# Moving the transposes of x's second quarter behind the first weight unit

## The chip, the cores and the metric

One Trainium2 chip, one of its cores. The metric is device time in microseconds of one launch. TensorE (PE in the profile) multiplies and transposes into the eight PSUM banks; VectorE (DVE) and ScalarE (ACT) work on tiles in SBUF and PSUM; SyncE (SP) issues nearly all loads from HBM; GpSimd (POOL) issues a few small ones. All numbers are f32; matrix products are split in a high and a low part so that three products in fp32r stand for one in f32.

## The reference

A two-layer trunk on x (256 tokens, 2048 channels) with a condition vector c (2048). What matters here is its beginning:

```python
cond = jax.nn.silu(c)
for l in range(DEPTH):                                    # DEPTH = 2
    mod = (cond @ w_ada[l] + b_ada[l])[:, None, :]        # w_ada[l]: 2048 x 12288
    sh1, sc1, g1, sh2, sc2, g2 = jnp.split(mod, 6, axis=-1)
    u = x * (1.0 + sc1) + sh1
    y = even_mixer(u, w_in_ab, ...) if l % 2 == 0 else odd_mixer(u, w_qkv, ...)
    x = layer_norm(ALPHA * x + (1.0 + g1) * y, ...)
    u = x * (1.0 + sc2) + sh2
    y = conv_ffn(u, w_up[l], conv_w[l], conv_b[l], w_down[l])
    x = layer_norm(ALPHA * x + (1.0 + g2) * y, ...)
```

`even_mixer` begins with `z = u @ w_in` (2048 x 5136) and ends with `@ w_out`; between them are a pooling mixer and gated linear attention. So the first weights can be multiplied once the matching channels of u are there, and these need x transposed (channels on partitions) and the sums over all 2048 rows of w_ada for the shift and scale of those channels.

## The kernel before

**Weight units.** All large weights are streamed in units of 4 x 128 rows and 512 columns (1 MB, two loads of 512 KB), through four raw slots. For each unit ScalarE writes a rounded high part (`hi_unit`, L557), VectorE the rest as low part (`lo_unit`, L889), each in two slots, and TensorE does 16 products with the high part (8 with u's high and 8 with u's low part) and 8 with the low part (`unit`, L1353). A unit is a column chunk c and a quarter j of the 2048 rows. The front has 48 units (32 of w_in in `IN_ORDER`, 16 of w_out). Units 0, 1, 2 are quarter 0 of three chunks (banks 0/1, 2/3, 4/5), units 3, 4, 5 are quarter 1 of the same, so unit 3 is the first that needs u's channels 512 to 1023.

**Pieces of u.** x is loaded in four quarters (`load_x`, L484), each 512 KB. A piece v is 256 channels: two pieces to a quarter of x. TensorE transposes a piece (`x_T`, L1601) into bank 7, ScalarE copies it to SBUF (`x_piece`, L614) and later writes u's high part (`u_piece`, L619), VectorE u's low part (`u_first`, L940). Since all pieces share bank 7, a transpose waits for the copy of the piece before.

**Sums over w_ada.** The 24 "pairs" of `ADA_PAIRS` are 1024 columns of w_ada each, 16 rows (r) of 128 x 1024 loaded one by one, 512 KB each, into eight slots. Row r of a pair is multiplied by silu(c) and added up, by VectorE (`ada_row`, L896), or for rows 0 to 11 of pairs 0 and 1 by TensorE (`ada_rows`, L1439): pair 0 in banks 4 and 5, pair 1 in banks 6 and 7, which VectorE reads as it folds in row 12 (L902). `ada_sum` (L1419) then sums over partitions on TensorE into bank 6, and `ada_evac` (L912) adds the bias: pair n gives shift and scale of u's quarter n (n below 4). Pairs 2 and 3 are spread over units 3 to 14, two or three rows a unit (`ada_plan`, L144); pairs 4 and 5 are the first gate's.

**Order around the change.** Each engine's program is in order and written out by hand.

- SyncE: pair 0's rows with x's first quarter after row 3; units 0 and 1; pair 1's rows 0 to 7; unit 2; x's second quarter; pair 1's rows 8 to 15; units 3 to 6 and so on, each followed by the rows that `ada_plan` gives to the unit four before (L499 to L526). A row's load waits until its slot was used by TensorE or VectorE (`load_row`, L405). The load of unit u waits for `lo_unit` of u - 4 (L418), counted from unit 4. Behind unit 9, once the second set of parameter rows is transposed, goes the first gate's bias (`gate_load`, L457): a broadcast of 1 MB into the tile that shares its place with those rows. Behind unit 10 follow the small low-rank gate weights (L516 to L519).
- TensorE: pair 0's rows, pieces 0 and 1, sum of pair 0, then unit 0, pair 1's rows 0 to 7, unit 1, rows 8 to 11, unit 2, pieces 2 and 3, sum of pair 1 (L1700 to L1774), unit 3, unit 4, `rows_T` (L1591) into bank 7, and on. Pieces 4 and 5 follow unit 7, 6 and 7 follow unit 10.
- ScalarE: pieces 0 and 1, high parts 0 and 1, u pieces 0 and 1, high parts 2 and 3, pieces 2 and 3, u pieces 2 and 3, high part 4, and on (L639 to L712).
- VectorE: pair 0, u pieces 0 and 1, low parts 0, 1, 2, pair 1's rows 12 to 15, low part 3, evacuation of pair 1's sum, u's low pieces 2 and 3, low part 4, then low part s + 2 and the rows of unit s for each s (L1215 to L1287).

Elsewhere `layer_norm` and `mlp` follow, and the second layer with attention; none of it is touched.

Of the kernel before, what the change touches and what calls it, by code (L numbers as in the profile page):

```python
# [14 lines left out]
S = 256  # L15
P = 128
F = 5504
KT = D // P
# [171 lines left out]
def build(nc, A, out):  # L190
# [7 lines left out]
    with ctx:  # L198
# [110 lines left out]
        def sem(name):  # L309
            if name not in sems:  # L310
                sems[name] = ctx.enter_context(nc.semaphore(name))
            return sems[name]
# [16 lines left out]
        def ada_slot(m, r):  # L329
# [2 lines left out]
                return r % ADA_FIRST, 2 * m + r // ADA_FIRST + 1  # L332
            return r % ADA_SLOTS, 8 + (m - 4) * (KT // ADA_SLOTS) + r // ADA_SLOTS + 1

        def pe_rows_at(m):
            return pair[2 + m]

# [66 lines left out]
        def _(sp):  # L404
# [94 lines left out]
            for v in range(FRONT_UNITS):  # L499
                c, j = IN_ORDER[v] if v < IN_UNITS else OUT_ORDER[v - IN_UNITS]  # L500
                load_quarter(v, w_in if v < IN_UNITS else w_out, c, j)
                if v == 1:
                    for r in range(ADA_FIRST):
                        load_row(1, r)
                if v == 2:
                    load_x(1)
                    for r in range(ADA_FIRST, KT):
                        load_row(1, r)
                if v in (6, 8):
                    load_x(2 + (v == 8))  # L510
                if v == 9:
                    sp.wait_ge(sem("rows_T"), 2)
                    gate_load(0, 2, 0)
                if v == 10:
                    sp.wait_ge(u_ready, 2 + U_FIRST + 2)
                    sp.dma_start(w_lr[:, :, :], A["w_in_ab"][0][:, OFF_LR:OFF_LR + GRANK].rearrange(  # L516
                        "(k p) n -> p k n", p=P)).then_inc(sem("lr_in"), 16)
                    sp.dma_start(w_g[0:GRANK, :], A["w_gate_lr"][0]).then_inc(sem("gla_in"), 16)
                    sp.dma_start(w_g[GRANK:GRANK + 1, :], A["b_gate"][0:1, :]).then_inc(sem("gla_in"), 16)  # L519
                if v == 20:  # L520
                    sp.wait_ge(a_step, A0 + 4 * KT)
                    sp.dma_start(sums_in[:, :], A["sums"]).then_inc(sem("pool_in"), 16)
                    sp.dma_start(band[:, :, :], A["band"]).then_inc(sem("pool_in"), 16)
                    for g in range(4):
                        sp.dma_start(w_pool[:, g], A["w_pool"][0, g].rearrange("(k p) n -> p k n", p=P)
                                     ).then_inc(sem("pool_in"), 16)  # L526
# [29 lines left out]
        def _(act):  # L556
# [56 lines left out]

            def x_piece(v):  # L614
                act.wait_ge(sem("xT_full"), v + 1)
                nc.scalar.activation(xT[:, 2 * v:2 * v + 2, :], bank[7].rearrange("p (k s) -> p k s", k=2), ACT.Copy
                                     ).then_inc(sem("xT_out"), 1)

            def u_piece(v):  # L619
# [19 lines left out]
            for v in range(2):  # L639
                x_piece(v)  # L640
            hi_unit(0)
            hi_unit(1)
            for v in range(2):
                u_piece(v)
            for s in range(FRONT_UNITS):
                if s == 2:
                    for v in (2, 3):
                        x_piece(v)
                    for v in (2, 3):
                        u_piece(v)  # L650
                hi_unit(s + 2)
# [228 lines left out]
        def _(dve):  # L880
# [332 lines left out]

            out_tail = y_out((0, "out"), True, True, OUT_BANKS, {c: s for s, c in OUT_LAST.items()})
            for s in range(FRONT_UNITS):  # L1215
                if s == 2:
                    ada_evac(1, 0)
                    u_first(1)
                    lo_unit(s + 2)
                    continue  # L1220
                if s in (13, 17):
# [25 lines left out]
                        mix_lo(v)  # L1247
                if s in OUT_LAST:
                    out_tail(OUT_LAST[s])
                if s == 1:  # L1250
                    beside(s)
                if s < FRONT_UNITS - 1:
                    lo_unit(s + 2)
                if s == GATE_SLOT + 1:
# [97 lines left out]
        def _(pe):  # L1352
# [247 lines left out]

            def x_T(v):  # L1601
                pe.wait_ge(sem(f"x_in{v // 2}"), 16)
                if v:
                    pe.wait_ge(sem("xT_out"), v)
                for k in range(2):
                    for t in range(NT):
                        ins = nc.tensor.transpose(bank[7][:, k * S + t * P:k * S + (t + 1) * P],
                                                  x[:, t, (2 * v + k) * P:(2 * v + k + 1) * P], ident)
                ins.then_inc(sem("xT_full"), 1)

# [89 lines left out]
            for u in range(FRONT_UNITS):  # L1700
                if u < IN_UNITS:
                    c, j = IN_ORDER[u]
                    b = PART_BANKS[c] if j < 2 else FULL_BANKS[c]
                    first, last, piece = j % 2 == 0, j % 2 == 1, U_FIRST + 2 * j
                    if j == 0 and PART_CHUNKS.index(c) >= 3:
                        pe.wait_ge(sem("z_part"), PART_CHUNKS.index(c) - 2)
                    if j == 2:
                        n = FULL_CHUNKS.index(c)
                        if n < 2:
                            pe.wait_ge(sem("z_part"), 7 + n)  # L1710
                        else:
                            pe.wait_ge(sem("z_done"), n - 1)
                else:
                    c, j = OUT_ORDER[u - IN_UNITS]
                    b = OUT_BANKS[c]
                    first, last, piece = j == 0, j == 3, U_MIX + 2 * j
                    if j == 0:
                        pe.wait_ge(*((sem("z_done"), 7 + c) if c < 2 else (sem("gla_st"), GH) if c == 2 else
                                     (acc_free, 2 + PH[0, "out"]["chunk"] + 1)))
                unit(u, [(k, 4 * j + k) for k in range(4)], (uhi, ulo), first, last, bank[b:b + 2], piece=piece,  # L1720
                     by_tile=Y_LAST[(0, "out"), 3] if u == FRONT_UNITS - 1 else None)
                if u == 0:
                    pe.wait_ge(sem("xT_out"), 2)
                    pe.wait_ge(a_out, 2)
                    ada_rows(1, 0, ADA_FIRST)
                if u == 1:
                    ada_rows(1, ADA_FIRST, PE_ROWS)
                if u in (2, 7, 10):
                    if u == 2:
                        pe.wait_ge(a_step, A0 + KT + PE_ROWS + 1)  # L1730
                    if u == 7:
                        pe.wait_ge(sem("cols_in"), 2)
                    for v in {2: (2, 3), 7: (4, 5), 10: (6, 7)}[u]:
                        x_T(v)
                if u == 4:
                    pe.wait_ge(sem("rows_in"), 16 * 14)
                    pe.wait_ge(sem("xT_out"), 4)
                    rows_T(2, 14, bank[7])
                if u == LR_SLOT:
                    pe.wait_ge(sem("lr_lo"), 1)  # L1740
                    pe.wait_ge(sem("xT_out"), 8)
                    low_rank(0, 12)
                if u == LR_SLOT + 1:
                    low_rank(12, KT).then_inc(sem("lr"), 1)
                if u == GATE_SLOT:
                    pe.wait_ge(sem("lr_out"), 1)
                    pe.wait_ge(sem("gla_in"), 32)
                    pe.wait_ge(sem("z_part"), 6)
                    for t in range(NT):
                        ins = nc.tensor.matmul(T[t][:, :], lrT[0:GRANK + 1, t * P:(t + 1) * P], w_g[:, :],  # L1750
                                               start=True, stop=True)
                    ins.then_inc(sem("gate_pre"), 1)
                if u in HEAD_S1:
                    if u == 21:
                        pe.wait_ge(sem("log_a"), 1)
                        pe.wait_ge(sem("pool_in"), 16 * 6)
                        pe.wait_ge(sem("z_done"), 2)
                    gla_T(HEAD_S1[u])
                if u in HEAD_S2:
                    gla_scores(HEAD_S2[u])  # L1760
                if u in HEAD_S3:
                    gla_values(HEAD_S3[u])
                for g in POOL_MEAN.get(u, ()):
                    pool_mean(g)
                for g in POOL_MAP.get(u, ()):
                    pool_map(g)
                for v in Y_B_T.get(u, ()):
                    pe.wait_ge(sem("y_b"), v - 3)
                    if v == 5:
                        pe.wait_ge(a_out, 1 + SUM_NO[5, 1] + 1)  # L1770
                    channels_T(lambda t, k: z[:, t, OFF_Q + (k - 8) * P:OFF_Q + (k - 7) * P], bank[7 - v % 2], T_MIX, v)
                if u == 39:
                    pe.wait_ge(t_free, 2 + T_MIX + 8)
                beside(u)  # L1774
# [118 lines left out]
```

## Time and profile before

| | us |
|---|---|
| median of 3 runs | 2323.1 (2319.01 to 2328.11) |
| profiled execution, its own time | 2321.39 |
| its span | 2319.6 |
| PE busy | 2244.5 (97%) |
| DVE busy | 1698.1 (73%) |
| ACT busy | 1006.6 (43%) |
| DMA, mean | 264 GB/s |

In the timeline a line has the start, the duration, the engine, the line of the kernel, the operation with the tiles written and read, their shapes, how many instructions were merged (x), and in brackets how long the engine was idle before and what released it. Times are from the span's start. SPq is SyncE's queue: the duration of a DMA there is the time of its issue alone; the time to its landing is in the view of the DMAs, counted from the issue. In the view of stretches a row has start:end, length, the busy time and instructions of PE, PEld, DVE, ACT and POOL, then TensorE's granted clock as a share of 2.4 GHz, the DMA's busy share and GB/s.

### The profile page before, as it was taken

To read this page: it belongs to the slowest core of one execution; us is meant where nothing else is said; L and a number is where in the kernel's file an instruction comes from. 1 tells how busy PE (TensorE), PEld (TensorE's weight loads), DVE (VectorE), ACT (ScalarE), POOL (GpSimd) and SP (SyncE) were. 2 spreads that over 40 slices of the span, in tenths; PEclk is the share of its full clock that TensorE was granted. 3 is DMA by queue.
4 is the path that set the end of the run, shared out by engine and by line. 5 is a ranking of instruction groups with operands and counts; after the bars stand their busy time and mean duration, and the time that the engine had idled before them with its cause. 6 is when DMAs were issued, how large, how long until landed. Compare 5 with 4: busy or idle time off the path is not lost. (4 is left out here: it accounts for less than half of the span.)

```text
span 2319.6 us, 28131 instructions
## 1 busy us (share of the span) xinstructions
PE 2244.5 (97%) x11321; PEld 1880.4 (81%) x11321; DVE 1698.1 (73%) x1672; ACT 1006.6 (43%) x1001; POOL 8.3 (0%) x19
## 2 busy tenths in 40 slices
PE   7899999999999999999999999999999999999996
PEld 3777777788888888888878888887888888888885
DVE  3799889959977778788887667775599645656555
ACT  1445343354443344453355444434544434444432
POOL 1000000000000000000000000000000000000000
PEclk9999999999999999999999999999999999999998
DMA  9999688958778988879967777774688556565553
GB/s 374 362 405 344 242 295 316 346 178 309 276 259 308 306 284 274 283 265 322 341 232 288 272 253 277 276 246 147 219 289 298 205 195 204 185 196 185 192 192 125
DMA packets 392227, 612.66 MB, mean 264 GB/s; under 512 B 21113, under 2 KB 205073, under 8 KB 390562
## 3 DMA queue, kind: packets, MB, share of 16 engines
q1 hardware_dynamic: 389378, 608.42, 74.9%
q10 hardware_dynamic: 2272, 2.20, 0.3%
q8 instruction: 89, 1.46, 0.2%
q0 software_dynamic: 448, 0.25, 0.0%
q14 instruction: 40, 0.33, 0.0%
HBM read 608.70 MB, written 2.10 MB: 263 GB/s over the span
## 5 line engine op out<-in xcount | busy, mean ns | idle before, releaser
L893 DVE TENSOR_TENSOR w_lo<-w_raw,w_hi 128x2048 fp32r<-128x2048 f32 x380 | 847.7, 2232 | 415.8 <-ACT w_hi L562 349.3
L562 ACT ACTIVATE w_hi<-w_raw 128x2048 fp32r<-128x2048 f32 x380 | 710.3, 1870 | 859.2 <-PE banks L1370 520.6
L1486 PE MATMUL banks<-u_hl,w_hi 128*128 128x512 f32 x2368 | 576.6, 392 | 8.7 <-DVE g_sum L1102 6.9
L1486 PEld LDWEIGHTS banks<-u_hl,w_hi 128*128 128x128 f32 x2368 | 432.6, 188 | 96.1 <-DVE g_sum L1102 9.4
L1370 PE MATMUL banks<-w_hi,u_hl 128*128 128x512 f32 x1920 | 481.5, 404 | 11.7 <-ACT u_hl L624 5.9
L1370 PEld LDWEIGHTS banks<-w_hi,u_hl 128*128 128x128 f32 x1920 | 365.1, 193 | 96.4 <-issue 17.3
L1494 PEld LDWEIGHTS banks<-u_hl,w_lo 128*128 128x128 f32 x2368 | 308.6, 191 | 14.5
L1494 PE MATMUL banks<-u_hl,w_lo 128*128 128x256 f32 x2368 | 313.0, 283 | 0.0
L1370 PE MATMUL banks<-w_hi,hid_hi 128*128 128x512 f32 x688 | 269.7, 392 | 0.0
L1370 PE MATMUL banks<-w_hi,hid_lo 128*128 128x512 f32 x688 | 267.8, 389 | 0.0
L909 DVE SCALAR_TENSOR_TENSOR ada_acc<-ada_w,silu_c,ada_acc 128x1024 f32<-128x1024 f32 x187 | 239.2, 1279 | 18.8 <-DMA ada_w<-in_w_ada 12.2
L1370 PE MATMUL banks<-w_lo,u_hl 128*128 128x512 f32 x960 | 238.6, 391 | 3.1 <-DVE w_lo L893 3.1
L1370 PEld LDWEIGHTS banks<-w_lo,u_hl 128*128 128x128 f32 x960 | 180.5, 188 | 41.5 <-DVE w_lo L893 3.9
L1370 PE MATMUL banks<-w_lo,hid_hi 128*128 128x512 f32 x688 | 171.9, 389 | 0.0
L1370 PEld LDWEIGHTS banks<-w_hi,hid_hi 128*128 128x128 f32 x688 | 129.2, 188 | 27.6 <-issue 1.0
L1370 PEld LDWEIGHTS banks<-w_hi,hid_lo 128*128 128x128 f32 x688 | 129.2, 188 | 27.6 <-issue 1.0
L1370 PEld LDWEIGHTS banks<-w_lo,hid_hi 128*128 128x128 f32 x688 | 129.1, 188 | 26.8
L909 DVE SCALAR_TENSOR_TENSOR ada_acc_aux<-ada_w,silu_c,ada_acc_aux 128x1024 f32<-128x1024 f32 x75 | 95.9, 1279 | 2.1 <-DMA ada_w<-in_w_ada 1.1
L792 ACT ACTIVATE conv<-conv 128x512 f32<-128x512 f32 (+1 forms) x44 | 27.4, 623 | 135.8 <-DVE conv L1121 135.8
L909 DVE SCALAR_TENSOR_TENSOR ada_acc_alt<-ada_w,silu_c,ada_acc_alt 128x1024 f32<-128x1024 f32 x52 | 66.7, 1282 | 7.0 <-DMA ada_w<-in_w_ada 3.7
L1121 DVE SCALAR_TENSOR_TENSOR conv<-g_sum,cols,conv 128x255 f32<-128x255 f32 (+1 forms) x148 | 64.9, 479 | 1.3
L586 ACT ACTIVATE g_sum<-banks 128x512 f32<-128x512 f32 (+1 forms) x38 | 22.3, 586 | 97.4 <-PE banks L1494 97.4
(211 smaller groups left out, 1271.8 us busy)
## 6 DMA issues: line engine op xcount, KB each, us to landing
ada_w<-in_w_ada SPq DMA_DIRECT2D x352, 512.0 KB, 6.8
w_raw<-in_w_up SPq DMA_DIRECT2D x344, 512.0 KB, 4.6
w_raw<-in_w_down SPq DMA_DIRECT2D x152, 512.0 KB, 4.7
w_raw<-in_w_qkv SPq DMA_DIRECT2D x96, 512.0 KB, 4.7
w_raw<-in_w_in_ab SPq DMA_DIRECT2D x64, 512.0 KB, 8.8
ada_w_more<-in_w_ada SPq DMA_DIRECT2D x32, 512.0 KB, 10.3
w_raw<-in_w_out_ab SPq DMA_DIRECT2D x32, 512.0 KB, 5.3
w_raw<-in_w_o SPq DMA_DIRECT2D x32, 512.0 KB, 5.1
```

What stands on the lines that cost most here:

```text
L562: nc.scalar.activation(whi[:, u % HL_SLOTS, 0:width], raw[:, u % RAW_SLOTS, 0:width], ACT.Copy).then_inc(w_hi, 1)
L586: nc.scalar.activation(g_sum[:, 0:nf, :], pair[b // 2][:, 0:nf, S:2 * S], ACT.Copy).then_inc(g_low, 1)
L792: nc.scalar.activation(gc[:, 0:nf, :], gc[:, 0:nf, :], ACT.Gelu_apprx_tanh).then_inc(h_gelu, 1)
L893: nc.vector.tensor_tensor(wlo[:, u % HL_SLOTS, 0:width], raw[:, u % RAW_SLOTS, 0:width], whi[:, u % HL_SLOTS, 0:width].bitcast(f32), ALU.s ...
L909: nc.vector.scalar_tensor_tensor(acc[:, :], w, silu_c[:, r:r + 1], acc[:, :], ALU.mult, ALU.add).then_inc(a_step, 1)
L1121: ins = nc.vector.scalar_tensor_tensor(gc[:, k, lag:S], src, cols[:, at:at + 1], gc[:, k, lag:S], ALU.mult, ALU.add)
L1370: return nc.tensor.matmul(banks[t][:, 0:width], u_at(kt, t), w[:, slot, k * width:(k + 1) * width], start=start, stop=stop)
L1486: ins = nc.tensor.matmul(bank[banks[s] + i][:, :], tile(whi, k, s, i), uhl[:, kt].rearrange("p a s -> p (a s)"), start=first and k == 0, s ...
L1494: ins = nc.tensor.matmul(bank[banks[s] + i][:, S:2 * S], tile(wlo, k, s, i), uhi[:, kt, :], start=False, stop=last and k == len(kts) - 1)
```

## The change

Pieces 2 and 3 of x are transposed right behind unit 0, ahead of pair 1's rows, into banks 4 and 5 (`x_bank`), without a wait for the copies of the pieces before; TensorE waits for their copies before unit 2, which accumulates in those banks. ScalarE copies them ahead of high part 2, and writes u pieces 0 and 1 ahead of high part 1. On VectorE the evacuation of pair 1's sum and u's low pieces 2 and 3 go ahead of low part 3. The wait for bank 7's release by VectorE goes from unit 2 to the parameter rows behind unit 4. The gate's bias is loaded behind unit 18 (and the rows of unit 14, the last of pair 3) and not behind unit 9.

```diff
--- before.py
+++ after.py
@@ -332,6 +332,9 @@
                 return r % ADA_FIRST, 2 * m + r // ADA_FIRST + 1
             return r % ADA_SLOTS, 8 + (m - 4) * (KT // ADA_SLOTS) + r // ADA_SLOTS + 1
 
+        def x_bank(v):
+            return T[v - 2] if v in (2, 3) else bank[7]
+
         def pe_rows_at(m):
             return pair[2 + m]
 
@@ -508,7 +511,7 @@
                         load_row(1, r)
                 if v in (6, 8):
                     load_x(2 + (v == 8))
-                if v == 9:
+                if v == 18:
                     sp.wait_ge(sem("rows_T"), 2)
                     gate_load(0, 2, 0)
                 if v == 10:
@@ -613,7 +616,7 @@
 
             def x_piece(v):
                 act.wait_ge(sem("xT_full"), v + 1)
-                nc.scalar.activation(xT[:, 2 * v:2 * v + 2, :], bank[7].rearrange("p (k s) -> p k s", k=2), ACT.Copy
+                nc.scalar.activation(xT[:, 2 * v:2 * v + 2, :], x_bank(v).rearrange("p (k s) -> p k s", k=2), ACT.Copy
                                      ).then_inc(sem("xT_out"), 1)
 
             def u_piece(v):
@@ -639,13 +642,14 @@
             for v in range(2):
                 x_piece(v)
             hi_unit(0)
-            hi_unit(1)
             for v in range(2):
                 u_piece(v)
+            hi_unit(1)
             for s in range(FRONT_UNITS):
-                if s == 2:
+                if s == 0:
                     for v in (2, 3):
                         x_piece(v)
+                if s == 2:
                     for v in (2, 3):
                         u_piece(v)
                 hi_unit(s + 2)
@@ -1213,9 +1217,11 @@
 
             out_tail = y_out((0, "out"), True, True, OUT_BANKS, {c: s for s, c in OUT_LAST.items()})
             for s in range(FRONT_UNITS):
-                if s == 2:
+                if s == 1:
+                    beside(s)
                     ada_evac(1, 0)
                     u_first(1)
+                if s in (1, 2):
                     lo_unit(s + 2)
                     continue
                 if s in (13, 17):
@@ -1247,8 +1253,6 @@
                         mix_lo(v)
                 if s in OUT_LAST:
                     out_tail(OUT_LAST[s])
-                if s == 1:
-                    beside(s)
                 if s < FRONT_UNITS - 1:
                     lo_unit(s + 2)
                 if s == GATE_SLOT + 1:
@@ -1600,11 +1604,11 @@
 
             def x_T(v):
                 pe.wait_ge(sem(f"x_in{v // 2}"), 16)
-                if v:
+                if v and v not in (2, 3):
                     pe.wait_ge(sem("xT_out"), v)
                 for k in range(2):
                     for t in range(NT):
-                        ins = nc.tensor.transpose(bank[7][:, k * S + t * P:k * S + (t + 1) * P],
+                        ins = nc.tensor.transpose(x_bank(v)[:, k * S + t * P:k * S + (t + 1) * P],
                                                   x[:, t, (2 * v + k) * P:(2 * v + k + 1) * P], ident)
                 ins.then_inc(sem("xT_full"), 1)
 
@@ -1722,19 +1726,20 @@
                 if u == 0:
                     pe.wait_ge(sem("xT_out"), 2)
                     pe.wait_ge(a_out, 2)
+                    x_T(2)
+                    x_T(3)
                     ada_rows(1, 0, ADA_FIRST)
                 if u == 1:
                     ada_rows(1, ADA_FIRST, PE_ROWS)
-                if u in (2, 7, 10):
-                    if u == 2:
-                        pe.wait_ge(a_step, A0 + KT + PE_ROWS + 1)
+                    pe.wait_ge(sem("xT_out"), 4)
+                if u in (7, 10):
                     if u == 7:
                         pe.wait_ge(sem("cols_in"), 2)
-                    for v in {2: (2, 3), 7: (4, 5), 10: (6, 7)}[u]:
+                    for v in {7: (4, 5), 10: (6, 7)}[u]:
                         x_T(v)
                 if u == 4:
                     pe.wait_ge(sem("rows_in"), 16 * 14)
-                    pe.wait_ge(sem("xT_out"), 4)
+                    pe.wait_ge(a_step, A0 + KT + PE_ROWS + 1)
                     rows_T(2, 14, bank[7])
                 if u == LR_SLOT:
                     pe.wait_ge(sem("lr_lo"), 1)
```

## Rows read from the trace of the kernel before

**Rows 1.** The page: span, and the DMA's busy share in 40 slices.

```profile
span 2319.6 us, 28131 instructions
...
DMA  9999688958778988879967777774688556565553
```

**Rows 2.** Stretches of 10 us; columns as in the heading line, granted clock third from last.

```profile
60.00:70.00 10.00, 5.73 (x29) 5.22 (x27) 4.47 (x7) 3.93 (x5) 0.00 (x0) 0.68 1.05 406
110.00:120.00 10.00, 9.96 (x47) 8.04 (x45) 8.40 (x6) 4.80 (x4) 0.00 (x0) 1.00 1.04 396
140.00:150.00 10.00, 9.05 (x40) 6.86 (x39) 9.76 (x14) 6.71 (x9) 0.00 (x0) 1.00 1.05 408
270.00:280.00 10.00, 10.00 (x46) 6.70 (x45) 8.52 (x17) 1.92 (x1) 0.00 (x0) 1.00 0.54 191
```

**Rows 3.** The timeline, 60 to 78 us: start, duration, engine, line, tiles, idle before.

```profile
61.92 1.91 ACT L562 ACTIVATE w_hi<-w_raw 128x2048 fp32r<-128x2048 f32 x1 [12.20 <-DMA w_raw<-in_w_in_ab]
...
64.46 1.09 PE L1607 MATMUL banks<-consts,x_tok 128*128 128x128 f32 x4 [3.03 <-ACT x_T L616]
...
65.34 3.41 PE L1435 MATMUL banks<-consts,ada_acc_alt 128*128 128x1 f32 x16
...
68.87 0.15 DVE L925 SCALAR_TENSOR_TENSOR mod<-banks,cols 128x4 f32<-128x4 f32 x1
69.06 2.08 ACT L624 ACTIVATE u_hl<-x_T,mod 128x256 fp32r<-128x256 f32 x4 [2.88 <-DVE mod L925]
...
70.29 5.52 PE L1370 MATMUL banks<-w_hi,u_hl 128*128 128x512 f32 x16 [1.54 <-ACT u_hl L624]
...
77.46 3.79 PE L1370 MATMUL banks<-w_hi,u_hl 128*128 128x512 f32 x16
```

**Rows 4.** The timeline of SyncE's DMA issues, 20 to 110 us.

```profile
37.21 1.68 SPq L485 DMA_DIRECT2D x_tok<-in_x  x1
44.79 1.90 SPq L415 DMA_DIRECT2D ada_w<-in_w_ada  x4
...
66.18 0.88 SPq L420 DMA_DIRECT2D w_raw<-in_w_in_ab  x2
...
84.20 0.34 SPq L460 DMA_DIRECT2D gate<-in_b_ada  x1
...
94.25 8.18 SPq L518 DMA_DIRECT2D w_gate<-in_w_gate_lr  x1
...
102.84 1.21 SPq L420 DMA_DIRECT2D w_raw<-in_w_in_ab  x2
```

**Rows 5.** Issue to landing: x's second load alone, then all weight loads to 100 us.

```profile
x_tok<-in_x SPq DMA_DIRECT2D x1, 512.0 KB, 11.9
...
DMA to landing us min/median/max: 3.9/10.5/13.0
```

**Rows 6.** The timeline, 30 to 61 us.

```profile
30.32 1.95 PE L1435 MATMUL banks<-consts,ada_acc 128*128 128x1 f32 x16 [1.01 <-DVE ada_acc L909]
...
43.69 1.92 PE L1446 MATMUL banks<-ada_w,silu_wide 128*32 128x512 f32 x16
...
47.27 3.92 PE L1370 MATMUL banks<-w_hi,u_hl 128*128 128x512 f32 x16
...
59.70 1.30 PE L1370 MATMUL banks<-w_lo,u_hl 128*128 128x512 f32 x5
59.72 1.28 DVE L909 SCALAR_TENSOR_TENSOR ada_acc_alt<-ada_w_more,silu_c,ada_acc_alt 128x1024 f32<-128x1024 f32 x1
```

**Rows 7.** The timeline, 110 to 150 us.

```profile
110.93 2.67 DVE L909 SCALAR_TENSOR_TENSOR ada_acc<-ada_w_more,silu_c,ada_acc 128x1024 f32<-128x1024 f32 x2 [4.67 <-DMA ada_w_more<-in_w_ada]
...
113.52 2.28 DVE L893 TENSOR_TENSOR w_lo<-w_raw,w_hi 128x2048 fp32r<-128x2048 f32 x1
...
117.55 1.98 PE L1370 MATMUL banks<-w_lo,u_hl 128*128 128x512 f32 x8
...
149.88 2.11 PE L1370 MATMUL banks<-w_lo,u_hl 128*128 128x512 f32 x8 [0.95 <-DVE w_lo L893]
```

## The prediction

> **What bounds the kernel now.** The page first: its span, 2319.6 us, and the DMA's row of tenths [rows 1]. Almost everywhere the DMA engines have room, but in the first slices (58 us each) they have none. The stretches show the same more closely [rows 2]: at 60 to 70 us TensorE is busy 5.7 of 10 us at a granted clock of 0.68 while the DMA moves 406 GB/s; at 140 to 150 us DMA and VectorE (9.8 of 10) are both full; by 270 us TensorE is full and the DMA half empty. So from some 250 us on, the end moves with TensorE's start, and whatever is won or lost ahead of that goes through to the end unless a wait behind it takes it up. At 406 GB/s one 512 KB load takes 0.524/0.406 = 1.29 us; this is the unit of the sums below.
>
> The stall that the change aims at stands in the timeline [rows 3]. Unit 2's last low product ends at 61.0 us, and so does VectorE's last row of pair 1 [rows 6]. The transposes of x pieces 2 and 3 share bank 7, and the copy of piece 2 queues on ScalarE behind the high part of weight unit 3, whose load has only just landed (61.92). So the second transposes start at 64.46, the sum of pair 1 behind them takes 3.41 us at the half clock, the scale is there at 69.02, and unit 3 starts at 70.29: 9.3 us after unit 2's end. Its 16 high products then take 5.52 us, since they too start at the half clock (3.92 for unit 1's [rows 6]).
>
> **What each part costs.** *The transposes move ahead of pair 1's rows.* This decides. x's second load is issued at 37.21 and lands 11.9 us later, at 49.1 [rows 4, 5]. It lies behind a full queue, and the change moves nothing ahead of it. TensorE ends unit 0 at 43.7 and takes pair 1's rows at once [rows 6]. With the change it stands before x_T(2), which waits for that load, and everything behind it on TensorE waits too: 49.1 - 43.7 = 5.4 us, more by 1.9 since unit 0 itself starts earlier (below). After such an idle time the clock will be at the lower level, as at 64.46, where four transposes took 1.09 us [rows 3]: two pieces are 2.2 us, until 51.3.
>
> Then follow TensorE's own steps. Eight rows of pair 1: before from 43.69 to 47.27, 3.6 us, plus 0.9 if the first two run at half clock: 55.8. Unit 1: high part 3.9, low part 1.98 with 0.2 of overlap [rows 6, 7], 5.7: 61.5. Four rows, half of the 3.6: 63.3. Unit 2, 5.7: 69.0. VectorE takes rows 12 to 15 from 63.6 at 1.28 to 1.33 us each [rows 6] and is done at 69.0 as well. The sum takes 1.95 us at the full clock [rows 6]: 71.0. Evacuation 0.25, then 1.2 from the scale to unit 3's first product (69.02 to 70.29): 72.5. Unit 3 at the full clock is 5.7 again, so unit 4 starts near 78.3, where it started at 77.46 [rows 3]. TensorE's whole gain from the shorter sum, the full clock and the missing wait for ScalarE is thus used up by the wait for x: net +0.8 us. With transposes at the full clock and no slow rows it would be -1.2.
>
> *The queue behind those rows.* SyncE issues in order, and its next loads (rows 8 to 15 of pair 1) wait until TensorE has used rows 0 to 7. The first is now issued at 44.79, 1.1 us after TensorE's start [rows 4, 6], while the queue still has work to 49.1. With the change it is issued at 51.3 + 1.1 + 0.5 (one row more slowly) = 52.9, into an empty queue. An almost empty queue took at least 3.9 us to land a load [rows 5], so it lands at 56.8, where by the pace it landed at 49.1 + 1.29 = 50.4. Every load behind it is 6.4 us later; with no slow clock 4.8.
>
> The Trainium skill, DMA: Bandwidth & Descriptors, "Anatomy of one DMA", gives for another queue kind 2.0 us plus bytes over 436 GB/s, an estimate of 3.2 us for this load. By it the delay would be 0.7 us less; the row's 3.9 is what I use.
>
> *The sum ahead of unit 3's low part.* lo_unit(3) now stands on VectorE behind the sum's evacuation and four u parts. These end 2.8 us after the scale, so the low part ends at 71.2 + 2.8 + 2.3 = 76.3, just before unit 3's high products end. TensorE does not wait. But SyncE's load of unit 7 waits for it: 66.18 before [rows 4], 76.3 now. The delayed queue runs to 50.4 + 16 x 1.29 + 6.4 = 77.4 (16 loads lie between), so the new load lands at 76.3 + 3.9 = 80.2 and its second half at 81.5, against 50.4 + 18 x 1.29 = 73.6: the delay grows to about 8.
>
> *The gate rows.* Their load is 1 MB, two loads' time, 2.6 us, taken out of the queue at 84.2 [rows 4]. Delay 5.4. The old queue had holes in this stretch too: from 73.6 to the small gate weights lie 21 loads and one of a quarter of the size, by the pace 27.4 us, so 101.0, but SyncE, held by the 8.18 us issue ahead of unit 11's load, was free only at 102.4 [rows 4]. Of these 1.4 us, or with the last landing twice as much, some may be caught up: 2.6 to 5.4 of delay are left at unit 11's load. I take the middle, 4.0. At the new place, behind unit 18's load, the 2.6 us fall on rows of pair 4, two to a unit and needed beside the low-rank products, which cover them; without that cover they cost up to 2.6. I take 0.
>
> *ScalarE's order.* u pieces 0 and 1 go ahead of unit 1's high part: unit 0 starts 1.9 us sooner, and the time ends in the wait for x. Copies of pieces 2 and 3 now hold unit 2's high part until about 52; unit 2 starts at 63.3. Banks 4 and 5 are free by then, so the new wait before unit 2 costs nothing. All zero.
>
> *Where the delay surfaces.* VectorE at 110.93 has waited 4.67 us for a row of pair 2, and the low part of unit 10 behind it ends at 115.80; TensorE wants it at 117.55 [rows 7]. That is 1.75 of slack, plus the 0.8 above: a delay of 4.0 costs TensorE another 1.4 there. At 149.88 there is none: TensorE waits 0.95 for VectorE already [rows 7], and between the two the DMA is full [rows 2]. So the whole delay is through by unit 15. **Sum:** +4 us on the profiled execution's 2321.4. The median of the runs is 1.7 above that; on it, 2327. What a measurement of this kernel can tell from no change is about 0.5%, 11.6 us.
>
> **Rivals.** *The stall simply goes* (0.22). If the wait for x is shorter than its row says or the hole in the queue is caught up by 110 us, only the quicker sum and the clock are left: unit 3 would start at 61.0 + 1.95 + 0.25 + 1.2, but not before high part 3 (63.83) and its u piece (1.1), so near 65 to 66, 4 to 5 us early: 2318.5. For it speaks that the 9.3 us gap is real. Against it speaks the landing at 49.1, which nothing in the change moves. The skill's DMA page ("Queues, rings and completion order") says that completion isn't in order of issue; the trace shows 11.9 us all the same.
>
> *A wash* (0.24). TensorE loses 0 to 1 at unit 3 and the queue's delay is caught up in its holes and by the gate rows: 2323 to 2324. Holes of that size are there from 75 to 90 us; but slack at unit 10 is 1.75 only.
>
> *Slower beyond noise* (0.06). VectorE's chain of rows carries the delay undiminished: 8 at unit 7, nothing caught up, and the gate's 2.6 us land between pair 4's rows while VectorE is full; a stall there long enough to drop the clock adds 1 to 2. 8 + 2.6 + 1.5 = 12 us: 2335. The point is unit 15's low part: it would have to come 8 us late, not 4. Against it: the gate's 1 MB does leave the queue before unit 10.
>
> *The gate move does nothing* (0.03). Were its load served beside the others at no cost, the delay stays at 8: 2331.
>
> My case holds 0.45. **How the numbers follow.** Cases of -5 to 0 us (0.46) and 3 to 8 (0.48) both lie within 0.5%. The range goes from the stall gone, 2318, to a delay of 8 with some scatter of the runs (they spread by 9 us), 2333; my own case's is 2324 to 2331. Faster by over 0.5% needs more than the stall holds: 0.03. Slower: 0.06.
>
> **What would show it.** Right: the first x_T(2) transpose at 49.1 or a little after, with TensorE idle from 42 at the half clock behind it; rows 8 to 15 issued near 53; GB/s falling for 2 to 5 us around 50 to 55; the sum at 2 us instead of 3.4; unit 3 starting at 71 to 73; low part 10 later than 118 and a wait for VectorE at units 10 to 15. Wrong: transposes at 44, no hole in the DMA's row, unit 3 at 66. If the hole is there but unit 15 is on time, the wash is right.

## The result and the profile after

| | kernel before | changed kernel |
|---|---|---|
| median of 20 runs each, us | 2321.93 | 2328.16 |
| ratio of the two | | 1.0028 (95%: 1.0019 to 1.0037) |
| profiled execution: own time, span, us | 2321.39, 2319.6 | 2328.41, 2326.6 |

The change costs 6.5 us, between 4.4 and 8.6 by the interval. That is slower beyond the runs' scatter, and inside half a per cent.

The page of the changed kernel, span and DMA's busy tenths, to set against [rows 1]:

```profile
span 2326.6 us, 28129 instructions
...
DMA  8999688958878988888967777774688556566553
```

The first slice has 8 where it had 9; of the others a few differ by one, either way. Stretches of the changed kernel (columns as in [rows 2]):

```profile
40.00:50.00 10.00, 2.37 (x12) 1.90 (x11) 0.00 (x0) 0.34 (x1) 0.00 (x0) 0.68 0.68 263
50.00:60.00 10.00, 10.00 (x54) 4.81 (x53) 2.29 (x1) 2.65 (x3) 0.00 (x0) 0.81 0.63 198
100.00:110.00 10.00, 8.66 (x43) 7.04 (x42) 9.61 (x7) 5.70 (x6) 0.00 (x0) 1.00 0.88 279
110.00:120.00 10.00, 8.50 (x38) 6.72 (x36) 5.73 (x4) 2.89 (x3) 0.00 (x0) 1.00 1.02 362
140.00:150.00 10.00, 8.07 (x36) 6.12 (x34) 9.58 (x11) 3.96 (x6) 0.00 (x0) 1.00 1.05 407
270.00:280.00 10.00, 10.00 (x48) 7.20 (x47) 8.43 (x12) 1.95 (x2) 0.00 (x0) 1.00 0.49 171
```

From 40 to 60 us the DMA moved 263 and 198 GB/s, where it has work for 406. At 110 to 120 TensorE is busy 8.5 us instead of 9.96. By 270 us all is as it was. Single microseconds show the hole itself:

```profile
46.00:47.00 1.00, 0.00 (x0) 0.00 (x0) 0.00 (x0) 0.00 (x0) 0.00 (x0) 0.50 0.38 145
48.00:49.00 1.00, 0.46 (x3) 0.49 (x4) 0.00 (x0) 0.00 (x0) 0.00 (x0) 0.50 0.01 2
52.00:53.00 1.00, 1.00 (x12) 0.22 (x8) 0.06 (x1) 0.91 (x1) 0.00 (x0) 0.50 0.00 0
53.00:54.00 1.00, 1.00 (x12) 0.29 (x8) 1.00 (x1) 0.00 (x0) 0.00 (x0) 0.59 0.50 74
```

From 46.4 us on only a trickle moves, the last 0.08 MB before 48.4, and then nothing until 53.2: some 7 us in which the DMA engines have next to no work. TensorE's granted clock is 0.50 there, its lower level. The timeline of the changed kernel, to set against [rows 3, 4, 6]:

```profile
48.54 1.94 PE L1611 MATMUL banks<-consts,x_tok 128*128 128x128 f32 x8 [7.63 <-DMA x_tok<-in_x]
...
50.41 3.59 PE L1450 MATMUL banks<-ada_w,silu_wide 128*32 128x512 f32 x16
...
52.37 2.55 SPq L418 DMA_DIRECT2D ada_w<-in_w_ada  x4
...
63.48 1.28 DVE L906 SCALAR_TENSOR_TENSOR ada_acc_alt<-ada_w_more,silu_c,banks 128x1024 f32<-128x1024 f32 x1 [8.25 <-PE banks L1450]
...
68.99 1.95 PE L1439 MATMUL banks<-consts,ada_acc_alt 128*128 128x1 f32 x16
69.21 1.91 ACT L565 ACTIVATE w_hi<-w_raw 128x2048 fp32r<-128x2048 f32 x1 [16.30 <-DMA w_raw<-in_w_in_ab]
...
71.05 0.15 DVE L929 SCALAR_TENSOR_TENSOR mod<-banks,cols 128x4 f32<-128x4 f32 x1
...
72.47 3.92 PE L1374 MATMUL banks<-w_hi,u_hl 128*128 128x512 f32 x16 [1.54 <-ACT u_hl L627]
...
76.27 0.88 SPq L423 DMA_DIRECT2D w_raw<-in_w_in_ab  x2
...
78.27 3.80 PE L1374 MATMUL banks<-w_hi,u_hl 128*128 128x512 f32 x16
```

TensorE stands 7.63 us until x lands (48.54), transposes at the lower clock, and only behind its rows can SyncE issue pair 1's rows 8 to 15: at 52.37, where it was 44.79. The sum takes 1.95 us and not 3.41, unit 3's high products 3.92 and not 5.52; and still unit 4 starts at 78.27 instead of 77.46. The load of unit 7 leaves at 76.27, 10 us later than before. It waits for unit 3's low part, and unit 3's weights themselves land only at 69.21 (61.92 before): 7.3 of the 10 us are the late queue, and VectorE's new order can account for 2.8 at most. Further on, against [rows 4, 7]:

```profile
99.40 7.89 SPq L521 DMA_DIRECT2D w_gate<-in_w_gate_lr  x1
...
107.70 0.91 SPq L423 DMA_DIRECT2D w_raw<-in_w_in_ab  x2
...
115.03 1.28 DVE L913 SCALAR_TENSOR_TENSOR ada_acc<-ada_w_more,silu_c,ada_acc 128x1024 f32<-128x1024 f32 x1 [3.90 <-DMA ada_w_more<-in_w_ada]
...
117.89 2.28 DVE L897 TENSOR_TENSOR w_lo<-w_raw,w_hi 128x2048 fp32r<-128x2048 f32 x1
...
120.23 2.13 PE L1374 MATMUL banks<-w_lo,u_hl 128*128 128x512 f32 x8 [1.73 <-DVE w_lo L897]
...
148.82 0.54 SPq L463 DMA_DIRECT2D gate<-in_b_ada  x1
...
149.97 3.93 PE L1374 MATMUL banks<-w_hi,u_hl 128*128 128x512 f32 x16 [1.93 <-ACT w_hi L565]
...
154.85 2.14 PE L1374 MATMUL banks<-w_lo,u_hl 128*128 128x512 f32 x8 [0.95 <-DVE w_lo L897]
```

VectorE waits 3.90 us for a row and ends low part 10 at 120.2; TensorE waits 1.73 us for it. The next wait that the kernel before did not have is at unit 15, 1.93 us for its high part (149.97); the 0.95 us ahead of its low products stood there before too. These start at 154.85, where they started at 149.88. The lag of 5.0 us then stands unchanged to 330 us.

### The profile page after: what moved, and what is told of

The parts are those of the page before. It is cut to its first block and busy times, and to the rows that moved or that the text cites. A ratio compares the mean times of both kernels' runs of the same rounds, so it can differ in the third digit from the quotient of the medians.

```text
span 2326.6 us, 28129 instructions
## 1 busy us (share of the span) xinstructions
PE 2244.9 (96%) x11321; PEld 1878.9 (81%) x11321; DVE 1698.4 (73%) x1672; ACT 1006.5 (43%) x1001; POOL 8.4 (0%) x19
```

## The experiments

All comparisons with the kernel before are from runs on the same chip. In the table, "unit 7" is the issue of its load, "GB/s" the DMA's mean from 40 to 80 us, "lag" the start of unit 15's low products less 149.88 (below zero: earlier than before), all three from one profiled execution; the ratio is that of all runs.

| kernel | unit 7 | GB/s | lag | ratio (95%) |
|---|---|---|---|---|
| before | 66.18 | 386 | 0 | 1 |
| changed | 76.27 | 309 | 5.0 | 1.0028 (1.0019 to 1.0037) |
| e1_x_early | 68.52 | 388 | -3.3 | 0.9991 (0.9982 to 0.9999) |
| e2_x_behind_rows | 69.69 | 371 | -1.3 | 0.9994 (0.9986 to 1.0003) |
| e3_unit3_fills | 76.37 | 311 | 5.3 | 1.0015 (1.0006 to 1.0025) |
| e4_gate_back | 76.70 | 308 | 7.6 | 1.0035 (1.0023 to 1.0047) |
| e5_gate_alone | 65.31 | 391 | -2.0 | 0.9995 (0.9984 to 1.0006) |
| e6_lo3_behind_sum | 71.69 | 356 | 3.1 | 1.0024 (1.0013 to 1.0036) |
| e7_x_early_lo3_ahead | 69.78 | 377 | 0.1 | 0.9989 (0.9978 to 1.0000) |
| e8_fill_and_lo3_first | 68.41 | 342 | 3.9 | 1.0006 (0.9996 to 1.0017) |
| e9_x_early_small_on_act | 73.25 | 364 | -2.2 | 0.9970 (0.9959 to 0.9980) |
| e10_small_on_act_alone | 65.83 | 394 | -2.9 | 0.9993 (0.9982 to 1.0003) |
| e11_changed_again | 78.81 | 310 | 7.2 | (one run) |
| e12_e9_lo3_ahead | 65.64 | 406 | -4.7 | 0.9982 (0.9971 to 0.9992) |

One caution on the single profiles. From 5 to 40 us the DMA moved 393 to 397 GB/s in most of them, but 372 in e7's and e11's, 379 in e8's and 366 in e9's. By that alone I estimate all that follows to be late: (394 - 372) x 35 / 406 = 1.9 us in e7 and e11, 1.3 in e8, 2.4 in e9. Their lags are to be read less by about so much; the profiles of e7, e8 and e9 are also each of the slowest run of their kernel.

**x earlier.** In SyncE's program, at unit 1 (and the load at unit 2 taken out):

```diff
                 if v == 1:
+                    load_x(1)
                     for r in range(ADA_FIRST):
                         load_row(1, r)
```

> The changed kernel, but x's second quarter is loaded ahead of pair 1's rows (right behind unit 1's weights) and not behind unit 2's. Theory (the wait for this load stalls TensorE and, through pair 1's rows, dries the load queue): x lands near 36 us, ahead of unit 0's end at 41; no idle wait ahead of the transposes, no hole in the DMA's row near 47 to 53, unit 3 starts at 65 instead of 72.5, the whole is 4 to 5 us faster than the kernel before (ratio 0.998) and 10 to 12 faster than the changed one. Rival (the new order on VectorE or the gate load's new place is what costs): the whole stays 5 to 7 us slower than before. Second rival (the early transposes cost only what TensorE idles, 7.6 us, of which most is covered): within 2 us of before.

The timeline of e1_x_early, TensorE's rows and SyncE's among them:

```profile
60.84 1.95 PE L1439 MATMUL banks<-consts,ada_acc_alt 128*128 128x1 f32 x16
...
64.72 5.49 PE L1374 MATMUL banks<-w_hi,u_hl 128*128 128x512 f32 x16 [1.94 <-ACT u_hl L627]
...
68.52 0.88 SPq L423 DMA_DIRECT2D w_raw<-in_w_in_ab  x2
...
71.86 3.79 PE L1374 MATMUL banks<-w_hi,u_hl 128*128 128x512 f32 x16
...
146.55 2.11 PE L1374 MATMUL banks<-w_lo,u_hl 128*128 128x512 f32 x8 [0.95 <-DVE w_lo L897]
```

The idle wait for x and the hole from 46 us on are gone; a short one stays at 68 to 70 us, where unit 7's load waits for the low part of unit 3. Unit 3 starts at 64.72, unit 4 at 71.86: 5.6 us ahead of the kernel before, a little more than expected. At unit 15's low products its lead is 3.3 us, and the whole gains 2.1 (0.2 to 4.2). So the late x is what makes the change slow; of the expected gain half is missing at the end. TensorE still leads by 5.4 us at unit 14's low products (137.67, before 143.04). It loses 2 us at unit 15, where it waits 1.95 us for the high part: VectorE, ahead of it in that chain, was only 3.3 us early, and had waited 4.8 us for rows of w_ada from 103 to 115 us, behind the hole that the small loads make (below).

**The transposes behind rows 0 to 7.** The calls of `x_T(2)` and `x_T(3)` change places with `ada_rows(1, 0, ADA_FIRST)`.

> The changed kernel, but TensorE does pair 1's rows 0 to 7 ahead of the two transposed pieces, so SyncE's next loads do not hang on x. Theory: TensorE still idles for x, from 44.5 to 48.5, but rows 8 to 15 are issued from 42 on and the queue never runs dry; unit 3 starts near 67.3, 3 us ahead of the kernel before; unit 7's load, held by the low part of unit 3, lands some 3 us later than before and the gate's move gives 2.6 back. Whole: 2 us faster than before (between 0 and 3.5). Rival (it is TensorE's idle time that costs, not the queue): 3 to 4 us slower than before, half of the changed kernel's loss.

The timeline of e2_x_behind_rows, TensorE's rows and SyncE's among them:

```profile
48.28 1.09 PE L1611 MATMUL banks<-consts,x_tok 128*128 128x128 f32 x8 [1.67 <-DMA x_tok<-in_x]
...
65.89 3.96 PE L1374 MATMUL banks<-w_hi,u_hl 128*128 128x512 f32 x16 [1.53 <-ACT u_hl L627]
...
69.69 0.88 SPq L423 DMA_DIRECT2D w_raw<-in_w_in_ab  x2
...
148.54 2.11 PE L1374 MATMUL banks<-w_lo,u_hl 128*128 128x512 f32 x8 [0.41 <-DVE w_lo L897]
```

TensorE waits 1.67 us for x, SyncE's rows go out in time, unit 3 starts 4.4 us early and the loss is gone: 0.9994. A hole remains, since unit 7's load waits for low part 3; the whole comes out near no change, 1.4 us faster (between 3.3 faster and 0.7 slower). TensorE's idle time shrank as well, so e2 alone doesn't separate it from the queue; e6 below does.

**Unit 3's weights fill the hole.** They are loaded behind `load_x(1)`, ahead of rows 8 to 15.

> The changed kernel, but unit 3's weights (1 MB, no wait in their way) are loaded ahead of pair 1's rows 8 to 15, so that they fill 2.6 us of the hole in the queue. TensorE's chain (wait for x, rows, units 1 and 2, sum) stays: unit 3 starts at 72.5 as in the changed kernel. Theory (the delay of the queue, surfacing at units 10 to 15, sets the loss): 2 to 2.6 us faster than the changed kernel, so 4 slower than before. Rival (TensorE's own chain up to unit 3 sets the loss): the same time as the changed kernel, 6 to 7 slower than before.

The timeline of e3_unit3_fills, TensorE's rows and SyncE's among them:

```profile
72.58 3.96 PE L1376 MATMUL banks<-w_hi,u_hl 128*128 128x512 f32 x16 [1.54 <-ACT u_hl L629]
...
76.37 0.88 SPq L423 DMA_DIRECT2D w_raw<-in_w_in_ab  x2
...
155.17 2.12 PE L1376 MATMUL banks<-w_lo,u_hl 128*128 128x512 f32 x8 [0.96 <-DVE w_lo L899]
```

By the profile the rival holds: unit 15 lags 5.3 us, as in the changed kernel. But it is not TensorE's chain either. The 2.6 us of filled hole came back as a second one: unit 7's load could not go before 76.37, and the mean from 40 to 80 us is 311 GB/s as it was 309. The median is 3.5 us above that of before (1.4 to 5.8), near the 4 of the theory and lower than the profile's lag, with an interval that overlaps that of the changed kernel: the median and the profile speak for different sides here.

**Both holes.** e3 with VectorE's low part of unit 3 ahead of pair 1's rows:

```diff
                 if s == 1:
+                    lo_unit(s + 2)
                     beside(s)
                     ada_evac(1, 0)
                     u_first(1)
+                    continue
```

> e3_unit3_fills with one thing more: VectorE does the low part of unit 3 ahead of pair 1's rows 12 to 15 (its high part is ready at 61.5 there), so that SyncE's load of unit 7 no longer waits for the sum to be read. In e3 the filled 2.6 us came back as a second hole, since unit 7's load went out at 76.4 as in the changed kernel. Theory (what is lost is the time that the load queue stands empty up to some 80 us, in however many holes, less the gate's 2.6): unit 7's load goes out near 66 to 68, the first hole keeps 4.3 us, and unit 15 is 1.7 us later than in the kernel before, against 5.3 in e3; the whole 1.5 to 3 us slower than before. Rival (TensorE's late start at unit 3 is enough): unit 15 stays 5 us late.

The timeline of e8_fill_and_lo3_first, TensorE's rows and SyncE's among them:

```profile
68.41 2.87 SPq L423 DMA_DIRECT2D w_raw<-in_w_in_ab  x2
...
81.54 3.79 PE L1378 MATMUL banks<-w_hi,u_hl 128*128 128x512 f32 x16
```

Unit 7's load went at 68.41, in an execution in which x landed 1.7 us later than in the changed kernel's. The lag of 3.9 less 1.3 for the slow head is 2.6, where theory said 1.7 and the rival 5; the whole is 1.4 us slower than before (-0.9 to 3.9). The median speaks for the theory. The profile can't decide: TensorE itself was 4.1 us late at unit 4 in that execution, and a lag of 3.9 at unit 15 is that lateness carried on.

**VectorE's order alone**, on the kernel before: evacuation and u pieces ahead of low part 3, as in the change.

> The kernel before with VectorE's order alone changed: pair 1's sum read and u's low pieces 2 and 3 ahead of the low part of unit 3. TensorE's unit 3 starts at 70.3 as before and does not wait for the low part (ready at 74, wanted at 75.6). But SyncE's load of unit 7 goes out at 74.1 and not 66.2, while the queue is empty at 69 to 71: everything behind is some 5 us late. Theory: 3 to 5 us slower than before, with a wait of TensorE for VectorE at unit 10. Rival (the queue catches up in its holes from 75 to 90 us): within 1 us of before.

The timeline of e6_lo3_behind_sum, TensorE's rows and SyncE's among them:

```profile
67.90 6.17 PE L1370 MATMUL banks<-w_hi,u_hl 128*128 128x512 f32 x16 [1.54 <-ACT u_hl L624]
...
71.69 0.88 SPq L420 DMA_DIRECT2D w_raw<-in_w_in_ab  x2
...
75.74 3.79 PE L1370 MATMUL banks<-w_hi,u_hl 128*128 128x512 f32 x16
...
152.95 2.11 PE L1370 MATMUL banks<-w_lo,u_hl 128*128 128x512 f32 x8 [0.96 <-DVE w_lo L893]
```

Unit 7's load 5.5 us late, 356 GB/s, unit 15 3.1 us late, the whole 5.6 us slower (3.0 to 8.4). This part, which I had given no cost of its own on TensorE and only the last 2 us of the queue's delay, costs by itself nearly as much as the whole change. This run separates the two engines most cleanly: unit 3 starts 2.4 us and unit 4 1.7 us earlier than in the kernel before (70.3 was expected for unit 3), so TensorE had a lead, and unit 15 is late all the same. The load queue set it. In e6 the queue is dry from 70 to 72 us. In the changed kernel it runs so late that this second hole is only a dip, to 209 GB/s at 76 to 77 us; e3, which shortens the first, opens it again. So the two costs don't add.

**The gate's load.** e4 puts it back behind unit 9 in the changed kernel (`if v == 9`), e5 moves it alone in the kernel before (`if v == 18`).

> The changed kernel, but the gate's bias is loaded behind unit 9 as before. Theory: its 2.6 us come back into the delayed queue ahead of unit 10: low part 10 and unit 15 are 2.6 us later than in the changed kernel, the whole is 8 to 9 us slower than the kernel before. Rival (the gate's place does not matter, holes of the queue take it up): as the changed kernel, 6 to 7 us slower. Second rival (its new place collides with pair 4's rows): 4 us slower than before, less than the changed kernel.

> The kernel before with the gate's load alone moved behind unit 18. Theory: the queue is 2.6 us ahead at unit 11, VectorE waits less for pair 2's last rows, but TensorE's start at unit 3 is unchanged, so only its waits at units 14 and 15 (0.4 and 0.95 us) can go: 0 to 1.5 us faster than before. Rival (the rows' queue sets TensorE's time there): 2.6 us faster. Rival (collision with pair 4's rows): 1 to 2 us slower.

Back at unit 9 it costs 2.6 us at unit 15 (7.6 against 5.0), as its bytes say. TensorE was 2.8 us later at unit 4 there than in the changed kernel, but it waits 1.32 us at unit 10 and 1.88 at unit 15, so that is not what sets unit 15. The whole is 8.1 us slower than before. Alone, it makes unit 15 2.0 us early, more than TensorE's two waits there (1.4), with 0.5 from an earlier unit 4 in that execution; on the whole 1.2 us, not told from nothing. So where the queue sets nothing, TensorE's place at unit 4 less these 1.4 us gives its place at unit 15.

**The sum's place with an early x.** e7 is e1 with the old order of `lo_unit(3)` on VectorE.

> As e1_x_early (x's second quarter loaded ahead of pair 1's rows), but with the low part of unit 3 ahead of the sum's evacuation on VectorE, as in the kernel before. With it unit 7's load goes out near 65.5 and not 69 to 70, but u's scale is read up to 2 us later. Theory (the load of unit 7 matters where the queue would run dry, and at 70 us it just does): 0 to 1 us faster than e1_x_early, 4 to 6 faster than before. Rival (the sum's reading decides, as the change says): 1 to 2 us slower than e1_x_early.

The timeline of e7_x_early_lo3_ahead, 63 to 76 us:

```profile
63.62 1.95 PE L1439 MATMUL banks<-consts,ada_acc_alt 128*128 128x1 f32 x16 [0.22 <-DVE ada_acc_alt L913]
65.52 1.91 ACT L565 ACTIVATE w_hi<-w_raw 128x2048 fp32r<-128x2048 f32 x1 [12.54 <-DMA w_raw<-in_w_in_ab]
67.46 2.29 DVE L897 TENSOR_TENSOR w_lo<-w_raw,w_hi 128x2048 fp32r<-128x2048 f32 x1 [3.90 <-ACT w_hi L565]
...
69.75 0.15 DVE L929 SCALAR_TENSOR_TENSOR mod<-banks,cols 128x4 f32<-128x4 f32 x1
...
71.17 5.01 PE L1374 MATMUL banks<-w_hi,u_hl 128*128 128x512 f32 x12 [5.61 <-ACT u_hl L627]
```

VectorE waits for unit 3's high part, so the scale is ready at 69.90, though the sum had ended near 65.6. TensorE waits 5.61 us. The whole takes the time of e1 all the same (2.6 us faster than before, 0.0 to 5.1, where 4 to 6 were expected). The queue would hide what TensorE loses, which e12 below tests.

**The small loads.** SyncE's three gate-weight loads go to ScalarE, behind pieces 4 and 5, `w_lr` last: in e9 on top of e1, in e10 alone.

```diff
+                if s == 7:
+                    act.wait_ge(u_ready, 2 + U_FIRST + 2)
+                    act.dma_start(w_g[0:GRANK, :], ...).then_inc(sem("gla_in"), 16)
+                    act.dma_start(w_g[GRANK:GRANK + 1, :], ...).then_inc(sem("gla_in"), 16)
+                    act.dma_start(w_lr[:, :, :], ...).then_inc(sem("lr_in"), 16)
```

> e1_x_early with the three small gate-weight loads issued by ScalarE behind unit 7's pieces and not by SyncE behind unit 10, where they held SyncE 8 us and emptied the queue. e1 was 5.6 us early at unit 4 and kept 3.1 at unit 15. Theory (the load queue bounds the stretch up to unit 15): with the hole near 100 to 105 gone unit 15 keeps 5 to 5.5 us, the whole is 4 to 5.5 us faster than before. Rival (VectorE's own work, 2 to 3 rows and a low part a unit, takes the lead away): 3 us at unit 15, the whole as e1, 2 faster than before.

> The kernel before with the three small gate-weight loads alone on ScalarE's queue. The hole near 102 to 105 us goes, which is 3 to 4 us of the queue, but TensorE has only its waits at units 14 and 15 (1.4 us) to gain: 1 to 2 us early at unit 15 as in e5_gate_alone, the whole 1 to 2 faster. Rival (nothing to gain): the same. If ScalarE's queue is served slowly and w_lr comes late, TensorE waits at unit 17: slower.

The stretch from 100 to 110 us, of the kernel before:

```profile
100.00:110.00 10.00, 8.65 (x43) 7.08 (x42) 6.04 (x4) 4.92 (x6) 0.00 (x0) 1.00 0.84 245
```

Of e9:

```profile
100.00:110.00 10.00, 8.64 (x42) 7.09 (x41) 9.09 (x7) 3.91 (x5) 0.00 (x0) 1.00 1.07 399
```

The hole that the 8.18 us issue made is gone. e9 is the best kernel of the study: 0.9970, 7.0 us faster than before (4.6 to 9.5), more than expected. Its profile is of its slowest run, with a slow head; less 2.4 its lead at unit 15 is 4.6 us by estimate. Alone the same edit gives 1.6 us, not told from nothing. In its profile unit 15 is 2.9 us early, more than the 1 to 2 expected, but unit 4 was 1.5 us early in that execution already: without an earlier TensorE there is little for the queue to feed.

**e9 with the old order**, to see whether the queue hid TensorE's loss in e7:

> e9_x_early_small_on_act with the low part of unit 3 ahead of the sum's evacuation on VectorE, as in the kernel before (e7 is the same edit on e1). There unit 3 started 3.8 us after the scale could have been read, because the low part waited for its weights, and yet e7's time was that of e1. Theory (in e1 and e7 the load queue bounds the stretch to unit 15 and hides TensorE's start; with the hole at 100 us gone TensorE's own lead counts): 2 to 4 us slower than e9, so 3 to 5 faster than before. Rival (the queue or VectorE still bounds it): the same as e9, 6 to 7 faster than before.

The timeline of e12, and its stretch from 100 to 110 us:

```profile
63.32 2.29 DVE L897 TENSOR_TENSOR w_lo<-w_raw,w_hi 128x2048 fp32r<-128x2048 f32 x1 [2.85 <-ACT w_hi L559]
...
67.02 5.54 PE L1374 MATMUL banks<-w_hi,u_hl 128*128 128x512 f32 x16 [4.55 <-ACT u_hl L621]
...
74.22 3.79 PE L1374 MATMUL banks<-w_hi,u_hl 128*128 128x512 f32 x16
...
100.00:110.00 10.00, 10.00 (x46) 8.27 (x45) 8.42 (x6) 3.37 (x3) 0.00 (x0) 1.00 1.07 393
```

Unit 3 starts at 67.02, 2.3 us behind e1's. The whole is 4.2 us faster than before (1.9 to 6.7), 2.8 less than e9, as theory said. Unit 4 at 74.22 is 3.2 us early; with the 1.4 us of waits gone that gives the 4.7 at unit 15, and VectorE waits for no load from 108 to 141 us. The same sum on e1's 5.6 us would give 7.0, e9's median. But e9's own profile doesn't show it (unit 4 only 1.0 us early, unit 15 2.2), and the intervals of e9 and e12 overlap, so this speaks for the theory more than it proves it.

**The changed kernel once more.**

> The changed kernel once more, for a second profile. In the first the lag behind the kernel before was 5.0 us from unit 15 to 330 us and 7.0 at the end; the 2 us more came with longer half-clock stretches at the layer norms (402 and 436 us). Theory: the lag at unit 15 is again 5 (within 0.5), the further 2 us are scatter of where half-clock stretches fall and come out otherwise, between -2 and +3. Rival: they are part of the change and come again as 2.

Lag at unit 15 7.2, less 1.9 for the slow head 5.3: as in the first. Behind it came another 2.7 us by the end, so this run does not rule the rival out. But between unit 15 and the end the other kernels moved against the same profile of before by anything from -3.7 (e3) to +4.7 us (e7), four of the eleven by +1 to +3. Whether that one profile was a lucky one behind unit 15 or kernels differ there isn't settled.

## Why the prediction was right

Forecast: 2327, no change beyond half a per cent, +4 us. Measured: 2328.16, +6.5 us. The two times are closer than the two changes by some luck: the forecast stood on the median of three runs, 2323.1, and over 20 runs it is 2321.93. Point by point:

- *The wait for x*: 49.1 forecast, 48.54 measured, idle 7.6 us. The transposes took 1.94 us (2.2). Right.
- *TensorE's chain*: unit 3 at 72.5, unit 4 at 78.3 forecast; 72.47 and 78.27 measured. The start of that execution was 0.3 us early, so this is closer than its terms.
- *The queue*: rows 8 to 15 at 52.9 forecast, 52.37 measured; unit 7's load at 76.3, measured 76.27. The first of these rows took 4.0 us to land (3.9). Right; e1 shows that this load of x is the cause, and e6 that a late queue costs TensorE time even when TensorE is early.
- *Where it surfaces*: a wait of 1.4 us at unit 10, measured 1.73, and the rest by unit 15. Right, though the wait of 1.93 us there was for the high part, where I had looked at the low one.
- *The gate's load*, 2.6 us: e4 shows 2.6. Its new place cost nothing that shows: 12.2 us to landing, first use at 220 us.
- *Mis-sized: "some may be caught up: 2.6 to 5.4 ... I take the middle, 4.0."* Measured 5.0 at unit 15. Nothing of note was caught up: the hole behind the small loads came again (279 GB/s from 100 to 110 us, 245 before), since it is made by an issue that waits for the queue to drain (7.89 us at 99.40, before 8.18 at 94.25) and moves with it; from 80 to 150 us both kernels moved 378 GB/s. The high end was the right one.
- *Not seen: that the reordering on VectorE was a cause of its own.* I worked out unit 7's late load, but as the last 2 us of a delay made by x. In the changed kernel it is no more than that (the dip at 76 us). e6 shows 3.1 us at unit 15 and 5.6 on the whole from it alone.
- The 1.5 us between the lag of 5.0 and the median's 6.5 lie within the interval and are open.
- The chances: the cases add up to 1 without the 0.03 for faster by over 0.5%, which belongs to no case.

The rival "the stall simply goes" had its number right for TensorE (4 to 5 us; e1 shows 5.6) and would still have been wrong on the whole: of the 5.6 us 3.3 are left at unit 15 and 2.1 (0.2 to 4.2) at the end.

A rule that I found after the runs, and that no further run tests: lag at unit 15 = bytes not moved from 40 to 80 us, over 406 GB/s, less 2.6 if the gate's load is later. Changed: (386 - 309) x 40 / 406 = 7.6, less 2.6 is 5.0 (5.0 measured). e6: 3.0 (3.1). e2: -1.1 (-1.3). e3: 4.8 (5.3). e1: -2.8 (-3.3). e4, with no gate term: 7.7 (7.6). With a slow head it falls short by 1.8 to 2.3: e11 4.9 (7.2), e7 -1.7 (0.1), e8 1.7 (3.9). It is not to be used where TensorE bounds, as in e5 (-3.1 by the rule and -2.0 measured) and e10, nor for e9 and e12, where the second hole, that of the small loads, is gone too.

## What to carry to other kernels

Where transfers bound a stretch, count the time that the load queue stands empty, not the time that an engine waits. A wait put in front of work that frees buffers goes into the queue: ask which loads, in program order, hang on the engine that will now stand still, and when the data it waits for lands. And a hole filled in one place comes back where the next load waits for something that did not move.

## What the runs showed of the hardware

- A queue that runs dry trickles out: behind x's load, the last in the queue of the changed kernel, the DMA moved its last 0.08 MB from 46.4 to 48.4 us, at 41 GB/s on the mean, and TensorE went on at 48.54. After that the first new bytes moved 0.8 to 1 us behind the issue at 52.37, and the load landed 4.0 us behind it.
- A load of many small pieces (`w_lr`) stopped SyncE for 8.18 us at its next issue, until the queue had all but drained (21 GB/s at 102 to 103 us, where the issue ends). Issued last on ScalarE's queue it took 0.40 us of that engine and 15.0 us to land beside the others, and the DMA kept 399 GB/s. The Trainium skill, DMA: Bandwidth & Descriptors, section "Queues, rings and completion order", says that each DMA engine takes turns between the queues it has work for; that w_lr landed while weights and rows moved on agrees.
- From 5 to 40 us executions differ, two of the changed kernel by 397 and 372 GB/s, all profiled ones by 366 to 397; I estimate up to 2.4 us from it on all that follows.
